# Four modulation chunks moved from VectorE in the first projection to GpSimd in the first attention

## What is computed

```python
for l in range(DEPTH):
    mod = jax.nn.silu(c) @ ada_w[l] + ada_b[l]
    sh_m, sc_m, g_m, sh_f, sc_f, g_f = jnp.split(mod, 6, axis=-1)
    hn = adaln(x, mix_norm_g[l], sh_m, sc_m)
    ... = jnp.split(hn @ w_in[l], IN_SPLITS, axis=-1)
    ...
    y = jnp.concatenate([o_a, o_b, o_c, o_d], axis=-1) @ w_out[l]
    x = x + g_m[:, None, :] * y
    hn = adaln(x, ffn_norm_g[l], sh_f, sc_f)
    ...
    x = x + g_f[:, None, :] * f
```

## Time and profile before

| | us |
|---|---|
| runs | 2112.98, 2115.78, 2106.33 |
| median | 2112.98 |
| the profiled execution's own time | 2110.77 |
| its span, from first to last instruction | 2109.1 |
| mean granted clock of TensorE | 0.977 of 2.4 GHz |

### The profile page before, as it was taken

How to read it: one execution, slowest core, us unless ns; L and a number is a source line. 1 busy time by engine, 2 the same in 40 slices (tenths; PEclk the granted TensorE clock), 3 DMA queues, 4 the chain that set the end, 5 groups by cost and what they waited for, 6 DMA issues and landing times.

```text
span 2109.1 us, 26253 instructions
## 1 busy us (share of the span) xinstructions
PE 2022.2 (96%) x9511; PEld 1659.9 (79%) x9516; DVE 1642.2 (78%) x2014; ACT 1342.5 (64%) x1862; POOL 66.0 (3%) x103
## 2 busy tenths in 40 slices
PE   8978999997899999999999999999999999999998
PEld 7756788885678888888888888888877887787886
DVE  5777777786769999999999999999986655556554
ACT  4354444445548888888888888888865445655443
POOL 0000000000000000000000000000000000000000
PEclk8988999998999999999999999999999999999999
DMA  9923588681159999999999999999985554424551
GB/s 397 376 80 135 196 313 312 259 305 66 63 213 386 371 384 372 385 372 388 375 377 389 369 386 365 386 372 389 411 331 219 181 194 152 154 78 160 180 193 47
DMA packets 83528, 584.16 MB, mean 277 GB/s; under 512 B 9440, under 2 KB 10080, under 8 KB 15184
## 3 DMA queue, kind: packets, MB, share of 16 engines
q1 hardware_dynamic: 71264, 516.98, 63.5%
q0 software_dynamic: 9696, 59.15, 7.4%
q10 hardware_dynamic: 2448, 6.42, 0.9%
HBM read 576.75 MB, written 5.77 MB: 276 GB/s over the span
## 4 chain that ended last, share of the span: by engine, by line
PE 88%; DVE 7%; DMA 2%; ACT 2%; issue 1%; POOL 0%; ACTq 0%; DVEq 0%
PE ps L677 27%; PE ps L653 17%; PE ps L655 17%; PE ps L654 17%; DMA Z<-in_ada 2%; PE ps L973 1%; PE ps L1167 1%; PE ps L935 1%; PE ps L783 1%; PE ps L598 1%; DVE ps L2319 1%; DVE xt_words L2348 1%; PE ps L709 1%; PE ps L950 1%; DVE weights_low L2087 0%
## 5 line engine op out<-in xcount | busy, mean ns | idle before, releaser
L2652 DVE TENSOR_TENSOR weights_low<-ring,weights_high 128x1024 fp32r<-128x1024 f32 x668 | 794.3, 1223 | 50.6 <-ACT weights_high L1762 41.8
L1762 ACT ACTIVATE weights_high<-ring 128x1024 fp32r<-128x1024 f32 x668 | 705.0, 1060 | 79.1 <-PE ps L655 64.2
L1371 ACT ACTIVATE weights_high<-ring 128x1024 fp32r<-128x1024 f32 x298 | 314.0, 1059 | 295.9 <-PE ps L677 206.4
L2087 DVE TENSOR_TENSOR weights_low<-ring,weights_high 128x1024 fp32r<-128x1024 f32 x298 | 361.8, 1223 | 166.3 <-ACT weights_high L1371 164.3
L653 PE MATMUL ps<-weights_high,xt_high 128*128 128x512 f32 x932 | 374.5, 402 | 2.3 <-DVE xt_low L2669 1.2
L655 PE MATMUL ps<-weights_high,xt_low 128*128 128x512 f32 x932 | 364.5, 391 | 0.0
L654 PE MATMUL ps<-weights_low,xt_high 128*128 128x512 f32 x932 | 363.7, 390 | 0.0
L653 PE MATMUL ps<-weights_high,hT_high 128*128 128x512 f32 x688 | 268.9, 391 | 1.2 <-DVE hT_low L2662 1.2
L655 PE MATMUL ps<-weights_high,hT_low 128*128 128x512 f32 x688 | 267.8, 389 | 0.0
L654 PE MATMUL ps<-weights_low,hT_high 128*128 128x512 f32 x688 | 267.7, 389 | 0.0
L677 PE MATMUL ps<-weights_high,xt_high 128*128 128x512 f32 x900 | 253.2, 404 | 0.9 <-ACT xt_high L1390 0.9
(11 more groups left out here) (300 smaller groups left out, 1585.8 us busy)
## 6 DMA issues: line engine op xcount, KB each, us to landing
ring<-in_stream SPq DMA_DIRECT2D x483, 1024.0 KB, 5.6
Z<-in_ada POOLq DMA_DIRECT2D x40, 1024.0 KB, 6.8
Z<-in_ada SPq DMA_DIRECT2D x4, 1024.0 KB, 11.4
result_store<-arena POOLq DMA_DIRECT2D x7, 512.0 KB, 7.7
ring<-in_ada SPq DMA_DIRECT2D x2, 1024.0 KB, 18.4
arena<-in_ada SPq DMA_DIRECT2D x2, 1024.0 KB, 25.4
Z<-in_dil POOLq DMA_DIRECT2D x1, 2048.0 KB, 9.8
Z<-in_na POOLq DMA_DIRECT2D x1, 2048.0 KB, 11.8
```

The costliest lines, as they stand in the source:

```text
L1371: act.activation(WH[:, p % SPLITS, :], ring[:, chunk % RING, half * PIECE:(half + 1) * PIECE], ACT.Copy).then_inc(hi_ready, 1)
L1762: act.activation(WH[:, slot, :], raw, ACT.Copy).then_inc(m["hi_ready"], 1)
L2087: nc.vector.tensor_tensor(WL[:, p % SPLITS, :], ring[:, chunk % RING, half * PIECE:(half + 1) * PIECE], WH[:, p % SPLITS, :].bitcast(F32), ...
L2652: nc.vector.tensor_tensor(WL[:, slot, :], raw, WH[:, slot, :].bitcast(F32), ALU.subtract).then_inc(m["lo_ready"], 1)
```

## The change

The projection sums only chunks 8 to 13 (`ADA_IN_GEMM` goes from 10 to 6, and `ADA_POOL` = 14 is new). Chunks 14 to 17 (half of one part, and half of the next) are summed by GpSimd. It loads 14 and 15 when `lam_exp_in` has come, and 16 and 17 behind the sums that free their slots. A new function `ada_sum` does a chunk with plain instructions: a half is multiplied by its column of `csilu` in place, and added to the accumulator (the first half of chunk 16 is multiplied into the accumulator, without an add), which makes eight multiplies and seven adds of 128x1024. The sum of 14 stands between the first and the second root of the attention, that of 15 between the second and the third, those of 16 and 17 behind the third. Loads 18 and 19 follow 16 and 17. The other constants that count from `ADA_MIX` keep their values.

```diff
-ADA_IN_GEMM = 10
-ADA_MIX = ADA_EARLY + ADA_IN_GEMM
+ADA_IN_GEMM = 6
+ADA_POOL = ADA_EARLY + ADA_IN_GEMM
+ADA_MIX = ADA_POOL + 4
...
-            for a in range(ADA_EARLY, ADA_MIX):
-                load_ada(a + ADA_RING)
+            def ada_sum(a):
+
+                acc, w = ada_acc[:, a // 4, :], ada_ring[:, a % ADA_RING, :]
+                q, at = a % 4, 2 * (a - ADA_POOL)
+                pool.wait_ge(ada_full[a % ADA_RING], 16 * ((a - ADA_EARLY) // ADA_RING + 1))
+                pool.wait_ge(ada_used, a)
+                for i in range(2):
+                    half, scale = w[:, i * D:(i + 1) * D], csilu[:, 2 * q + i:2 * q + i + 1]
+                    if q == 0 and i == 0:
+                        pool.tensor_scalar(acc, half, scale, None, ALU.mult).then_inc(ada_half, 1)
+                    else:
+                        pool.tensor_scalar(half, half, scale, None, ALU.mult).then_inc(ada_scaled, 1)
+                        pool.wait_ge(ada_scaled, at + i + (0 if a >= ADA_POOL + 2 else 1))
+                        if i == 1:
+                            pool.wait_ge(ada_half, a + 1 - ADA_EARLY)
+                        pool.tensor_tensor(acc, acc, half, ALU.add).then_inc(ada_half if i == 0 else ada_used, 1)
+
+            for a in range(ADA_EARLY + ADA_RING, ADA_POOL):
+                load_ada(a)
             pool.wait_ge(lam_exp_in, 1)
+            for a in range(ADA_POOL, ADA_POOL + ADA_RING):
+                load_ada(a)
             pool.memset(KI4, 0.0).then_inc(ki_cleared, 1)
             root(0, 4)
-            for b in range(NB):
-                root(4, 8)
+            ada_sum(ADA_POOL)
+            load_ada(ADA_POOL + 2)
+            root(4, 8)
+            ada_sum(ADA_POOL + 1)
+            load_ada(ADA_POOL + 3)
+            root(4, 8)
+            for a in range(ADA_POOL + 2, ADA_MIX):
+                ada_sum(a)
+                load_ada(a + ADA_RING)
             for a in range(ADA_MIX, ADA_FFN):
                 load_ada(a + ADA_RING)
...
-                    if g == 0 and p % 2 == 1:
+                    if g == 0 and p % 2 == 1 and ADA_EARLY + (p - SPLITS) // 2 < ADA_POOL:
                         ada_step(ADA_EARLY + (p - SPLITS) // 2)
```

More of the change, by code:

```diff
@@ L372, in program @@
         ada_full = [sem(f"ada_full{i}") for i in range(ADA_RING)]
-        ada_half, ada_used = sem("ada_half"), sem("ada_used")
+        ada_half, ada_used, ada_scaled = sem("ada_half"), sem("ada_used"), sem("ada_scaled")
         cols_in, unit_in, gates_in = sem("cols_in"), sem("unit_in"), sem("gates_in")
```

## The result

The change makes the kernel slower by 0.6%: the median goes from 2108.78 to 2122.43 us (12 runs of each), a ratio of 1.0062 with a 95% interval from 1.0047 to 1.0077. The profiled execution of after has a span of 2124.8 us, 15.7 more than the one of before, at a mean granted clock of 0.971 (0.977 before).

What follows compares the result with a forecast made beforehand. TensorE was taken to bound the projection and VectorE largely the attention. Terms -0.6 + 6.1 + 5.0 + 1.1 = +11.6 on the profiled 2110.77 gave 2122.4 us, range 2110 to 2131.

Steps and rivals of the forecast that it cites:

- Projection, -0.6: End of the first projection: VectorE's dropped steps gain only in the gap before 88.53, bounds 0 and 1.3, -0.6 us taken.
- Queues, 0: GpSimd's queue: moved loads 14 to 19 and the roots behind the sums delay nobody; cost 0.
- Price of GpSimd's instructions: GpSimd over 128x1024: multiply 0.95 us from the memset, add 2.3, one chunk's sum 6.5 (3.8 to 11.1).
- Sum 14, +6.1: Between first root and turn of A01: GpSimd's four instructions alternate with VectorE's, which are held for the whole sum; +6.1 us.
- Sum 15, +5.0: Behind the second root: 1.47 us hidden under PSUM inputs, the rest falls on rope, copies and second combination; +5.0 us.
- Sums 16 and 17, +1.1: Behind the third root: two products normalising A11 each meet a multiply, 1.9 us less 0.8 of VectorE's idle time; +1.1 us.
- The cover that was named: Rest of sums 16 and 17 costs 0, beside VectorE instructions with a PSUM input or MAX8 and replacement with one SBUF tensor.
- Clock, named and left out of the sum: TensorE from 125 to 133: after the pause, at 1.2 GHz, 8 us of work would take 13; a bound, not summed.
- Marks: Signs in the trace after: turn of A01 near 130.9, second root near 139.7, rope to first MAX8 near 10 us.
- the shadow: Rival, 120.43 to 124.38: GpSimd's work hardly holds VectorE; 2110.2 us without waits, 2114.3 with a third; chance 0.20.
- A larger gain in the projection with nothing paid: Rival: the whole gap before 88.53 closes and nothing is paid, 2109.5 us; chance 0.02.
- late: Rival: a sum takes over 13 us, delaying second and third roots and load 19; +27, 2138 us; chance 0.04.

Runs made afterwards that it cites:

- its copy with 10 matmuls: Kernel before plus ten matmuls that nobody reads, ahead of the scores of D00 in the first attention; ratio to before 1.0001 (0.9988 to 1.0014).
- the kernel with the last two sums: Changed kernel with only chunks 16 and 17 summed by GpSimd, 14 and 15 again by VectorE in the projection; ratio to before 1.0020 (1.0007 to 1.0033).
- the one with a pause: Kernel before plus 20 small linked VectorE products ahead of the combination of A00 and A01, GpSimd unchanged; ratio to before 1.0046 (1.0030 to 1.0063).
- the one-column kernel: Changed kernel with every GpSimd multiply and add cut to one of 1024 columns, loads and waits kept; ratio to before 0.9990 (0.9976 to 1.0004).
- the 16 matmuls: Changed kernel plus sixteen matmuls that nobody reads, ahead of the turn of A01 in the first attention; ratio to before 1.0048, once more 1.0060.
- the kernel with adds: Changed kernel with GpSimd's multiplies cut to one column and its seven adds whole; ratio to before 1.0044 (1.0029 to 1.0058).
- the kernel with multiplies: Changed kernel with GpSimd's adds cut to one column and its eight multiplies whole; ratio to before 1.0033 (1.0014 to 1.0052).

## Why the prediction was right, and where it was not

The sign, the size (+11.6 forecast; +13.7 between the medians) and the mechanism, a collision on the path, were right. That the time of 2122.4 us came out at 2122.43 is luck: the profiled execution from which it starts, 2110.77, lay 2.0 us above the median of the 12 runs of before, and the sum was 2.1 too small. The sum itself was less good than its result, since errors offset each other.

- **Projection, -0.6.** The first root comes 1.4 us earlier (117.94 against the earlier trace rows), of which 0.5 stood already at the load of chunk 12 (67.80 against 68.30), and the wait for chunk 13 before 88.53 is gone in this profile: the last gap is that before 81.68, where a low half comes behind the sum of chunk 12 (loaded at 67.80). Of the eight other profiles with this projection two have no such gap either, and in six one of 0.9 to 1.5 remains. From the load of chunk 12 to the first root, nine profiles with the changed projection take 49.3 to 51.6 us (mean 50.05); before takes 51.06, its copy with 10 matmuls 51.48, the kernel with the last two sums 50.98, and the one with a pause 55.56, at a granted clock of 0.94 from 80 to 110. A gain of about 1 is what the others give, within the bounds, but no more than the spread; it is not settled.
- **Queues, 0.** Right: the one-column kernel. The loads of 14 and 15 start at 101.14 (forecast near 102), and load 19 at 190.91, 20 us ahead of the step of chunk 18 at 211.36.
- **Price of GpSimd's instructions.** This step failed, in one term: the add was forecast at 2.3 and took 2.35, but the multiply was put at 0.95, from the memset, and took 2.85, above even the high end of 2.3. Here a pass that only writes was no measure for one that reads and multiplies. A sum takes 10.6 us, not 6.5.
- **Sum 14, +6.1: measured +4.1.** The step "all four fall into this stretch, and the stretch grows by the whole sum" failed. VectorE got past after three of the four turns, and a multiply holds it only in part of its length. The two errors, a sum too short (6.5 for 10.6) and a hold too complete, partly cancel, and leave 2.0 us too much.
- **Sum 15, +5.0: measured +5.7 in the first profile, +5.0 in the second, +4.9 to +5.7 in all.** Right for the same mixed reason.
- **Sums 16 and 17, +1.1: measured +0.3 from the bias of D00 to that of D10, and 0 to +0.6 between the biases of C00 and C10 (+0.4 in the first profile).** Only the first of the two products that normalise A11 was held (171.10 below, 0.42 when free), and VectorE's idle 0.5 us there took most of it. The cover that was named (inputs in PSUM, one SBUF tensor) held, but a plain multiply from SBUF to SBUF stands among those instructions. By the prediction's own words that kind is concerned, and it was left out: it lasts 0.52 in after, 0.82 with the 16 matmuls and 0.29 in before. VectorE's timeline in after, then that of before:

```profile
171.10 1.28 DVE L2423 TENSOR_TENSOR XN<-XN,rstd 128x256 f32<-128x256 f32 x1
...
190.25 0.52 DVE L2377 TENSOR_SCALAR FS<-xt_words 128x256 f32<-128x256 f32 x1
```

```profile
174.14 0.29 DVE L2350 TENSOR_SCALAR FS<-xt_words 128x256 f32<-128x256 f32 x1
```

- **Clock, named and left out of the sum.** This was the largest omission: 4.4 us to the bias of A11 and 2.9 from D10 to C00 in the first profile of after, 1.5 and 0.3 in the second. The bound worked out for it, 8 us of TensorE's work taking 13, was the right size for the first profile.
- **Marks.** The second root came at 140.41 (forecast 139.7), but of the 8.3 us by which it lies farther behind the first, the port made 4.1, and the rest lies in TensorE's stage behind the combination. The turn of A01 came at 127.10, not 130.9: of the difference 1.4 us is the earlier root, 2.0 the overestimate of sum 14, and in the rest the turn follows the combination at once (127.05) and not 0.4 behind it.

The sum as it should have read, for the first profile: port 4.1 + 5.7 + 0.3 + 0.4 = 10.5, clock 4.4 + 2.9 = 7.3, projection -1.4: +16.4. The step of chunk 18 lies 16.3 later than in the earlier trace rows, and the span is 15.7 longer.

*Of the rivals*, the shadow fell: short VectorE instructions don't go first, they wait for a whole add. Its test, a combination that stays at 0.35 us beside an add, could not be read, since in after the combinations met a multiply and kept their length. The 128x64 product beside the add (2.05 for 0.20) decided it, and so did two instructions of the combination's own size, 128x128 with two inputs in SBUF: the first index product of after (128.88, 0.80 for 0.35, beside an add that ends at 129.54) and the product in the kernel with adds (2.31 for 0.29). A larger gain in the projection with nothing paid fell with the total. GpSimd was never late: the load of 19 shows it.

On GpSimd's hold of VectorE, the measured rows are 2.05, 2.21 and 2.19 us beside adds of 2.35, and a hold of the first 1.2 us beside multiplies of 2.85. The Trainium skill (SBUF — State Buffer, "Who interferes with whom") says, of VectorE's two-port modes, that whoever issues first has the shared pair for the whole instruction. The adds agree. The multiplies don't: in the kernel with multiplies the copy at 140.23 and the combinations at 141.24 ran at their usual length beside one, and there the measurement decides. Why a multiply lets go in the middle was not found out.

## What to carry to other kernels

An engine that looks idle may be free only in part: here GpSimd's sums cost little where VectorE worked from PSUM or searched (two of them at most 1.8 us of the attention in one profile), while the other two, on the path beside instructions with SBUF inputs, made most of the loss. Price an engine's instruction by one of its own kind (a memset was a third of a multiply), and count what a late producer does to TensorE's clock in the stage behind: here 4 us of delay cost up to 4.5 more in the next stage, in another execution of the same kernel 1.5. One profile doesn't price that.

## What was not expected of the hardware

GpSimd's multiply with one tensor input is slower than its add with two: 2.85 against 2.35 us over 128x1024, while in one column they take 0.28 to 0.44 and 0.19 to 0.27. Such a multiply let VectorE's two-input instructions through after about 1.2 us, and held a plain copy again at its end (1.12 us for 0.29). And the same program, unchanged, was granted 0.50 from 120 to 135 in one execution and 0.76 in another, in which TensorE's pause was not shorter (3.82 against 3.35 us). Why was not found out.
